# Encoder kernel, feed-forward up projection: forms of u from two PSUM banks with twelve sums, and two reorderings on VectorE and ScalarE

## The reference

```
h = h + rmsnorm(mixed @ w_out, g_post_mix)
u = rmsnorm(h, g_pre_ffn)                      # 512 tokens x 1024 features
h = h + rmsnorm(conv_ffn(u, ...), g_post_ffn)

def conv_ffn(u, w_up, conv_w, conv_b, w_down):
    h = u @ w_up                               # 1024 x 5632: gate half and up half
    h = causal convolution of width 3 along the tokens, per channel, + conv_b
    gate, up = split(h, 2)
    return (gelu_tanh(gate) * up) @ w_down
```

## Time and profile before

| | |
|---|---|
| median of 3 runs | 853.69 us (853.6 to 855.11) |
| the profiled execution: time, span | 852.13 us, 850.3 us |
| PE busy in the span | 835.8 us, 98% |
| DVE, ACT, POOL busy | 652.0, 477.4, 399.8 us |
| chain that ended last | PE 87%, DVE 7%, DMA 2% |
| granted TensorE clock, mean | 0.997 |

### The profile page before, as it was taken

The page is one execution under the profiler, slowest core; times in us unless marked ns, Lnnn a source line. Parts: engine busy times, 40 slices in busy tenths (PEclk is TensorE's granted clock), DMA queues, the critical chain, the costliest instruction groups (busy, mean ns, idle before and its releaser), DMA issues.

```text
span 850.3 us, 13362 instructions
## 1 busy us (share of the span) xinstructions
PE 835.8 (98%) x4685; PEld 729.3 (86%) x4685; DVE 652.0 (77%) x1251; ACT 477.4 (56%) x898; POOL 399.8 (47%) x512
## 2 busy tenths in 40 slices
PE   8999999999999999999999999989999999999997
PEld 7888888888888888999998898879999999888885
DVE  6677787788766668965543589988888887799895
ACT  6566666877666654534452437365555554455562
POOL 5454434243333446986776427665555556100002
PEclk9999999999999999999999999999999999999999
DMA  7541233322223222343337432455544333745494
GB/s 218 164 126 51 71 80 95 94 78 80 82 81 81 63 62 65 110 137 100 88 123 255 142 125 85 157 167 167 167 120 118 118 118 119 278 162 195 151 290 156
DMA packets 138790, 109.24 MB, mean 128 GB/s; under 512 B 7559, under 2 KB 122191, under 8 KB 137700
## 3 DMA queue, kind: packets, MB, share of 16 engines
q1 hardware_dynamic: 137242, 101.00, 39.2%
q0 software_dynamic: 576, 4.19, 1.3%
q10 hardware_dynamic: 906, 3.20, 1.0%
HBM read 96.00 MB, written 12.37 MB: 127 GB/s over the span
## 4 chain that ended last, share of the span: by engine, by line
PE 87%; DVE 7%; DMA 2%; ACT 1%; POOL 1%; issue 1%; SPq 0%; DVEq 0%; ACTq 0%
PE banks L2234 22%; PE banks L2236 22%; PE banks L2235 22%; PE banks L2509 3%; PE banks L2511 3%; PE banks L2510 3%; PE banks L2410 2%; PE banks L2319 2%; PE banks L2318 2%; DVE wide L2060 2%; PE banks L2682 1%; PE banks L2681 1%; PE banks L2680 1%; PE banks L2382 1%; DMA ring_raw<-in_w_ffn_up_dram 1%; DVE pages L2001 1%
## 5 line engine op out<-in xcount | busy, mean ns | idle before, releaser
L845 POOL TENSOR_TENSOR ring_lo<-ring_raw,ring_hi 128x256 fp32r<-128x256 f32 x380 | 312.4, 854 | 271.5 <-ACT ring_hi L1001 271.2
L2234 PE MATMUL banks<-u_hi,ring_hi 128*128 128x512 f32 (+1 forms) x624 | 237.1, 380 | 2.5 <-DVE wide L2060 1.8
L2236 PE MATMUL banks<-u_hi,ring_lo 128*128 128x512 f32 (+1 forms) x624 | 232.2, 372 | 0.0
L2235 PE MATMUL banks<-u_lo,ring_hi 128*128 128x512 f32 (+1 forms) x624 | 232.0, 372 | 0.0
L2234 PEld LDWEIGHTS banks<-u_hi,ring_hi 128*128 128x128 f32 x624 | 118.1, 189 | 21.7 <-DVE wide L2060 2.0
L2236 PEld LDWEIGHTS banks<-u_hi,ring_lo 128*128 128x128 f32 x624 | 118.0, 189 | 20.9
L2235 PEld LDWEIGHTS banks<-u_lo,ring_hi 128*128 128x128 f32 x624 | 118.1, 189 | 18.6
L1001 ACT CAST ring_hi<-ring_raw 128x1024 fp32r<-128x1024 f32 x96 | 100.0, 1043 | 37.7 <-PE banks L2236 24.3
L2060 DVE SCALAR_TENSOR_TENSOR wide<-banks,cols,wide 128x511 f32<-128x511 f32 x88 | 64.8, 746 | 18.9 <-ACT wide L1361 11.4
L852 POOL TENSOR_SCALAR norm_ms<-norm_ss 128x1 f32<-128x1 f32 x15 | 6.0, 401 | 137.4 <-ACT pages L1011 137.3
L2234 PE MATMUL banks<-pages,ring_hi 128*128 128x512 f32 (+1 forms) x176 | 60.1, 341 | 0.0
(11 more groups left out here) (318 smaller groups left out, 1954.6 us busy)
## 6 DMA issues: line engine op xcount, KB each, us to landing
ring_raw<-in_w_ffn_up_dram SPq DMA_DIRECT2D x88, 256.0 KB, 3.4
ring_raw<-in_w_in_dram SPq DMA_DIRECT2D x60, 256.0 KB, 3.4
ring_raw<-in_w_ffn_down_dram SPq DMA_DIRECT2D x55, 256.0 KB, 3.4
ring_raw<-in_w_gate_dram SPq DMA_DIRECT2D x48, 256.0 KB, 3.2
ring_raw<-in_w_out_dram SPq DMA_DIRECT2D x16, 256.0 KB, 3.1
split_tokens<-pages SPq DMA_DIRECT2D x4, 1024.0 KB, 6.8
pages<-split_tokens POOLq DMA_DIRECT2D x4, 1024.0 KB, 11.9
second_tokens<-wide SPq DMA_DIRECT2D x10, 384.0 KB, 4.1
```

The source lines that it names most:

```text
L845: last = pool.tensor_tensor(wlo[:, r, c], raw[:, r, c], whi[:, r, c].bitcast(F32), ALU.subtract)
L2234: pe.matmul(out, lhs_hi, rhs_hi, start=start, stop=False)
L2235: pe.matmul(out, lhs_hi, rhs_lo, start=False, stop=False)
L2236: return pe.matmul(out, lhs_lo, rhs_hi, start=False, stop=stop)
```

## The change

1. **Forms of u.** Before, each half needed six of DVE's operations after u was complete: two sums high + low for u12 and u22 (L1987) and four differences. Now u12 and u22 are read from the PSUM banks in which u was turned (`turned_half`), so four operations remain (`t_forms_12`, `t_forms_34`), and they no longer wait for the last low part of u. Twelve sums and differences in all where there were sixteen. Half 0 and two of half 1 stand ahead of the first taps, the other two of half 1 between the taps of the first tile and the second.
2. **ACT** rounds each form of u as soon as it is there, half 0 ahead of the first unit's taps (before: after the first gelu) and half 1 after the first gelu (before: after the second).
3. **DVE** subtracts the low parts of the forms (`t_forms_low`) in the first step (before: in step 1).
4. **PE** waits for all eight of them before the first of the seven products of step 2 (before: ahead of the second), since that product writes bank 4.
5. **DVE, steps 2 to 9:** `up_edges(i)` stands ahead of `up_weight_sums(i + 1)`, where it stood behind.
6. **ACT, steps 2 to 9:** `up_forms_high(i + 1)` stands behind the gelu of the step's second unit, where it stood ahead of its taps; for step 2, ahead of `split_tokens(1)`.

```
+        T_RAW = {1: 1, 2: 3, 3: 0, 4: 2}
+        def turned_half(row, c):
+            banks = psum[:, 4:8, :].rearrange("p (t h) (k n) -> p h k t n", h=2, n=P)
+            return banks[:, row, 2 * c:2 * c + 2, :, :]
...
                 act.copy(psum[:, UP_BANK, 0:256], psum[:, W_BANK, 0:256]).then_inc(up_copied, 1)
-                if more:
-                    up_forms_high(i + 1)
                 act.wait_ge(up_edge, 2 * n + 2)
...
                 gelu(i, 1)
-            def t_forms_high(c):
-                act.wait_ge(t_form_sums, 6 * c + 10)
-                for q in range(1, 5):
-                    act.copy(t_form(q, slice(2 * c, 2 * c + 2))[0], u_raw(U_RAW[q], c)).then_inc(t_form_hi, 1)
-            for j in range(2):
-                ffn_unit(j, None, j)
-                t_forms_high(j)
+                if more:
+                    up_forms_high(i + 1)
+            def t_forms_high(c, which=(1, 2, 3, 4)):
+                for q in which:
+                    act.wait_ge(t_form_sums, 4 + 4 * c + q)
+                    act.copy(t_form(q, slice(2 * c, 2 * c + 2))[0], u_raw(T_RAW[q], c)).then_inc(t_form_hi, 1)
+            t_forms_high(0)
+            ffn_unit(0, None, 0)
+            t_forms_high(1)
+            ffn_unit(1, None, 1)
...
             gelu(1, 1)
+            up_forms_high(2)
             split_tokens(1)
-            up_forms_high(2)
...
-            def t_sums_rest(c):
...
+            def t_forms_12(c):
+                t1, t2, r11 = (u_raw(q, c).rearrange("p k (t n) -> p k t n", n=P) for q in (1, 3, 0))
+                dve.tensor_tensor(t1, turned_half(0, c), r11, sub).then_inc(t_form_sums, 1)
+                dve.wait_ge(t_form_sums, 5 + 4 * c)
+                dve.tensor_tensor(t2, turned_half(1, c), t1, sub).then_inc(t_form_sums, 1)
+            def t_forms_34(c):
+                r11, r21, t2 = (u_raw(q, c) for q in (0, 2, 3))
+                dve.wait_ge(t_form_sums, 6 + 4 * c)
+                dve.tensor_tensor(r11, t2, r11, sub).then_inc(t_form_sums, 1)
+                dve.tensor_tensor(r21, r21, t2, sub).then_inc(t_form_sums, 1)
...
-            dve.wait_ge(u_lo_done, 2 * TT)
-            t_sums_rest(0)
+            dve.wait_ge(t_form_sums, 4)
+            t_forms_12(0)
+            t_forms_34(0)
+            t_forms_12(1)
...
             ffn_taps(0, None, 0, (0,))
-            t_sums_rest(1)
+            t_forms_34(1)
             ffn_taps(0, None, 0, (1,))
+            t_forms_low(0)
             ffn_product(0, 0, first_tokens)
             ffn_taps(1, None, 1)
+            t_forms_low(1)
             ffn_product(1, 1, second_raw[:, 0:512])
             token_sums(0)
             for i in range(1, SEVEN_UP[-1] + 1):
                 ffn_taps(2 * i, i, 0, (0,))
-                if i == 1:
-                    t_forms_low(0)
-                else:
+                if i in SEVEN_UP:
                     up_forms_low(i)
                 ffn_taps(2 * i, i, 0, (1,))
                 ffn_product(2 * i, 0, first_tokens)
-                if i == 1:
-                    t_forms_low(1)
+                if i in SEVEN_UP:
+                    up_edges(i)
                 if i + 1 in SEVEN_UP:
                     up_weight_sums(i + 1)
-                if i in SEVEN_UP:
-                    up_edges(i)
                 ffn_taps(2 * i + 1, i, 1)
...
+                if n == 0:
+                    pe.wait_ge(t_form_lo, 8)
                 pe.wait_ge(w_lo_done, up_tile(i, 0) + 1)
                 one_of_seven(W_BANK, up_quarter(0, 0), quarter(0, 0)).then_inc(up_prod, 1)
-                if n == 0:
-                    pe.wait_ge(t_form_lo, 8)
-                else:
+                if n >= 1:
                     pe.wait_ge(up_edge, 2 * n)
```

More of the change, by code:

```diff
@@ L2000, in t_forms_low @@
                     hi, lo = t_form(q, slice(2 * c, 2 * c + 2))
-                    dve.tensor_tensor(lo, u_raw(U_RAW[q], c), hi.bitcast(F32), sub).then_inc(t_form_lo, 1)
+                    dve.tensor_tensor(lo, u_raw(T_RAW[q], c), hi.bitcast(F32), sub).then_inc(t_form_lo, 1)
             def up_weight_sums(i):
```

12 lines of the change are left out of this document (removed).

## The result

| | before | after |
|---|---|---|
| median of the runs, us | 853.64 | 844.49 |
| runs, us | 853.38 to 855.11 (4) | 844.18 to 844.87 (4) |
| profiled execution, us | 852.13 | 844.44 |
| its span, us | 850.3 | 842.6 |
| ratio after / before | | 0.9889, interval 0.9872 to 0.9907 |

The changed kernel is 9.15 us faster, where 7.3 was forecast.

The account below looks back on a forecast made before the run. PE was taken to be busy nearly throughout, waiting twice for DVE behind the start. 1.95 + 1.67 + 3.68 - 0 = 7.3 us off 852.13 gives 844.8, plus 1.6 to the median: 846.4; range 844.8 to 849.5.

Parts of the forecast that it names:

- First wait: PE's wait for DVE's taps of the second tile (L2060): goes, with its clock fall, for 1.95 + 1.67 = 3.62 us.
- The 1.67 us for the first fall: Three units after PE's restart at 522.76 took 34.37 us where 32.70 would do; the lowered clock costs 1.67 us.
- Second wait: PE's wait in step 2 for DVE's bank sum L2033: 3.11 us go once it stands ahead of the weight sums.
- ACT's list ends its catching up earlier: In step 2, the reason given for the 0.28 us in front of the third product to go too.
- Steps 3 to 9: PE waited for nothing here, so the change can only cost; forecast to keep 20.98 us per step, costing 0.
- x: Length of DVE's four weight sums in the ring of hand-overs from sixth product to next third product; forecast 3.5 us.
- bad end: The four weight sums take 4.30 us, as in step 2; each of seven passes costs 0.4 us, 2.8 in all.
- allowance: Ring of 11.1 + x against 15.0 us allowed from L2036 to the next step's third product: x may be 3.9 us.
- The low parts' cover: Steps 3 to 9: DVE's low parts of the weight forms come before the second product is due, cover 0.9 us.
- the rival that the ring binds: Steps 3 to 9: the ring of hand-overs closes late, up to 2.8 us back, 846.4 to 849.2; chance 0.22.
- The rival on the slower side: The ring binds and the clock falls in at least five of seven steps: 860.9 us; chance 0.04.
- The clock did not fall here: Said of step 2's products in the profile of before, which took 3.68 us too much, 3.11 before the last product.

Follow-up runs that it names:

- the trace without the fall: One more profile of the kernel before, no edit: 854.07 us; the clock did not fall behind the first wait.
- the stretched ring: Changed kernel with one, or two, extra DVE sums behind the weight sums of steps 2 to 8: 850.96 us with one, 855.38 us with two.
- the orders alone: Kernel before with items 5 and 6 alone, forms of u made as before: 847.29 us, ratio 0.9918.
- the forms alone: Changed kernel with items 5 and 6 taken back, items 1 to 4 kept: 848.84 us, ratio 0.9947 against before.

## Why the prediction was right, and where it was wrong

**First wait: right.** Second taps at 516.27 (forecast 516.7), the PSUM form at 0.68 us (0.70, bounds 0.61 to 1.05), six operations from 508.49 in some 4.1 us (4.1), wait and fall gone. The Trainium skill's page "VectorE: DVE Perf Modes", section "The TRN2 errata — SBUF-src ops pay a fixed extra latency per instruction", has the form from PSUM dearer by 0.06 us; the rows don't bear that out, with 0.68 from PSUM and 0.69 from SBUF. Taps for step 2 ended at 538.0 (538.2), the eight low parts near 530.3 (531), and no wait appeared in step 1 or 2. What I did not see is that the saved operations weren't needed: the new order does it without them.

**The 1.67 us for the first fall: right in the sum, wrong as a cause of its own.** I added 1.95 + 1.67 + 3.68, as if each stood by itself on the path. Between 523 and 569 us DVE was the late one, and the trace without the fall pays the same time as a wait of 1.61. The sum holds all the same, because it is all that PE lost up to step 3, and no new wait took its place: 7.35 measured against 7.3.

**Second wait: right that it goes, by a cure that works and isn't the only one.** "L2033 stands ahead of them" was to be the cure of the 3.11 us. It is one: with item 6 taken back the wait is gone all the same. But item 5 taken back alone costs 0.75 us, because the exchange on ACT ahead of `split_tokens(1)`, to which I gave only "ACT's list ends its catching up earlier" and 0.28 us, takes 2.6 of the 3.1 us by itself. I had read the wait at the operation named (L2033 behind four sums) and not asked why DVE came to those sums so late. It waited for ACT's taps, and they stood behind a rounding queue that began after a stand of 2.67 us. Both cures were shown with the new forms in place; neither ran alone on the kernel before.

**Steps 3 to 9: right.** x was 3.68 in even steps and 2.96 in odd ones, forecast 3.5 for all, bad end 4.30; allowance 3.9, shown by the stretched ring to 0.05 us. The low parts' cover too: forecast as gone at x = 3.5 + 0.9 = 4.4, so at 4.83 they should be 0.4 late, and PE waited 0.32. In the even steps only 0.2 us of x was left between this kernel and the rival that the ring binds, which I gave 0.22. The rival on the slower side needed the clock to fall in each step; it doesn't at 0.9 us.

**From the profile to the median: wrong, and this is the step that failed.** I took 844.8 for the profiled execution (844.44 measured) and added 1.6 us, because the profiled execution of before lay that much below its median. I carried this over whole, with no reason why the changed kernel should have it. Most of it was a part of what the change removes: in the two other profiles of before the clock also falls behind the second wait (1.7 and 2.6 us), and the one I had in hand was spared. The sentence "The clock did not fall here" was true of that execution and false of the kernel. Filling the waits gives 1.2 us on the median. The changed kernel has no such wait, and its profile and its median agree within 0.1 us: 844.49, where the term put 846.4.

The gain of 9.15 is 7.35 up to step 3, 1.2 for the clock behind the second wait, 0.3 for the stage's start, and 0.3 that the runs don't assign. The start lay within 0.1 us in the three profiles of before (495.98 to 496.08), but from 495.37 to 496.42 in the profiles of the kernels here, whose lists don't differ ahead of it, so I take its 0.3 for scatter.

The low end of the range failed by a smaller step of its own. 844.8 was the forecast for the profile with the 1.6 left out, and nothing was allowed below it, though it rested on a single profile. The 1.2 us don't explain that miss, since 853.69 - 7.3 - 1.2 = 845.2 lies inside the range; the 0.3 of the start and the 0.3 unassigned do. That the time fell just outside is in that part luck. But a wait of 3.11 us that spares the clock after one of 1.79 had lost it was reason enough to ask whether it always does.

## What to carry to other kernels

- When the profiled execution lies off the median, ask which waits in it could have gone otherwise before carrying the difference over as a constant. Here a wait whose fall of the clock was missing in that profile held 1.2 of the 1.6 us.
- Behind an engine that is late, walk back along its own list to the first place where it waited. The wait that PE shows names the last operation, and moving that ahead was one cure; the other was an idle of ACT further up the chain, which four roundings could fill. Undo each alone, and together, before saying which one did it.
- A ring of hand-overs worked out from start times was exact to 0.1 us. Adding a dummy operation to it is a cheap way to measure how much is left; here 0.2 us in the tighter steps.

## What the runs showed of the hardware

- **A fall of the clock varies between executions of one kernel.** Behind a wait of 1.79 us it fell in two of three profiles of before, and not in the orders alone; behind 3.1 us in two of three and in the forms alone; behind 4.2 us in the one profile with such a wait. Behind waits of 0.9 us or less in each of seven steps the mean clock stayed at 0.999.
- **Transposes of 0.115 us in the wait kept it up** in both kernels that had them, and narrow the spread of the runs from 4.5 to 0.7 us. They gained time (1.2 us) only where they ended before the wait did.
- **A sum or difference of DVE on 512 columns with one input in PSUM takes 0.68 us with POOL idle,** the same as one from SBUF with POOL idle (0.69). The ones with two inputs in SBUF go up to 1.22 to 1.27 beside POOL; the form with one in PSUM was not seen beside POOL on 512 columns, and on 256 columns it took 0.43 there (L2036 of the earlier trace rows, beside POOL in the earlier trace rows) and 0.42 or 0.43 in every step.
